# The out stage of a streaming-encoder block: VectorE forms the sums of m's blocks, and the low parts move between the additions

## The reference

```
merged = g_sb * y_sb + g_gla * y_gla
x = x + jnp.einsum('bsd,de->bse', merged, w_out[layer])
return _rmsnorm(x, g_final)
```

## Time and profile before

| | us |
|---|---|
| median of 3 runs | 820.55 (820.23 to 822.45) |
| the profiled execution, its own time | 820.71 |
| its span | 818.6 |
| TensorE busy, share of the span | 793.8, 97% |
| VectorE busy | 580.9, 71% |
| ScalarE busy | 410.5, 50% |
| GpSimd busy | 50.6, 6% |
| mean granted TensorE clock | 0.994 of full |

### The profile page before, as it was taken

How to read it: one execution, slowest core, us unless ns; L and a number is a source line. 1 busy time by engine, 2 the same in 40 slices (tenths; PEclk the granted TensorE clock), 3 DMA queues, 4 the chain that set the end, 5 groups by cost and what they waited for, 6 DMA issues and landing times.

```text
span 818.6 us, 11843 instructions
## 1 busy us (share of the span) xinstructions
PE 793.8 (97%) x4441; PEld 664.0 (81%) x4441; DVE 580.9 (71%) x811; ACT 410.5 (50%) x706; POOL 50.6 (6%) x44
## 2 busy tenths in 40 slices
PE   5999999999999999999999999999999999999896
PEld 5778888888888888879889888888888888888685
DVE  6528896989698698946645656665467776778865
ACT  8536675756666465655254153344343333465432
POOL 1630000000000000020000000000000000012500
PEclk9999999999999999999999999999999999999899
DMA  9852011112110220021110001234433344384222
GB/s 321 286 200 52 26 40 40 49 42 60 35 41 26 52 51 26 27 78 53 44 36 26 26 29 52 86 134 138 143 116 104 109 129 128 132 304 175 103 104 102
DMA packets 72483, 76.31 MB, mean 93 GB/s; under 512 B 3804, under 2 KB 57207, under 8 KB 71928
## 3 DMA queue, kind: packets, MB, share of 16 engines
q1 hardware_dynamic: 72386, 75.71, 28.8%
q10 hardware_dynamic: 54, 0.01, 0.0%
HBM read 55.79 MB, written 15.73 MB: 87 GB/s over the span
## 4 chain that ended last, share of the span: by engine, by line
PE 79%; DVE 10%; issue 5%; ACT 4%; POOL 1%; DMA 0%; DVEq 0%; ACTq 0%; POOLq 0%
PE pj L715 22%; PE tr L1019 5%; PE ob L967 5%; PE sc L967 5%; PE pj L859 4%; PE pj L1019 4%; PE ob L1019 4%; DVE surv L1680 4%; PE ob L807 3%; PE sc L1019 3%; PE pj L731 3%; PE tr L817 3%; PE pj L840 3%; PE sc L784 2%; PE tr L1077 2%
## 5 line engine op out<-in xcount | busy, mean ns | idle before, releaser
L715 PE MATMUL pj<-h_hi,w_lo 128*128 128x512 f32 x336 | 134.1, 399 | 0.0
L715 PE MATMUL pj<-h_hi,w_hi 128*128 128x512 f32 x336 | 133.8, 398 | 0.0
L715 PE MATMUL pj<-h_lo,w_hi 128*128 128x512 f32 x336 | 133.6, 398 | 0.0
L1680 DVE TENSOR_TENSOR_SCAN surv<-surv 128x128 f32<-128x128 f32 (+3 forms) x64 | 86.4, 1350 | 19.2 <-ACT beta L1186 18.7
L715 PEld LDWEIGHTS pj<-h_hi,w_lo 128*128 128x128 f32 x336 | 63.5, 189 | 12.1 <-issue 0.5
L715 PEld LDWEIGHTS pj<-h_lo,w_hi 128*128 128x128 f32 x336 | 63.3, 188 | 12.0 <-issue 0.3
L715 PEld LDWEIGHTS pj<-h_hi,w_hi 128*128 128x128 f32 x336 | 63.5, 189 | 11.7 <-issue 0.2
L1227 ACT ACTIVATE wt_hi<-tr 128x512 fp32r<-128x512 f32 (+2 forms) x96 | 43.6, 490 | 43.2 <-PE tr L817 41.7
L1603 DVE TENSOR_TENSOR w_lo<-w_raw,w_hi 128x1024 fp32r<-128x1024 f32 x33 | 40.3, 1221 | 26.7 <-ACT w_hi L1119 26.5
L1725 DVE TENSOR_TENSOR wt_lo<-tr,wt_hi 128x512 fp32r<-128x512 f32 (+2 forms) x96 | 50.0, 548 | 5.3 <-ACT wt_hi L1227 4.8
L1683 DVE TENSOR_TENSOR beta<-beta,surv 128x128 f32<-128x128 f32 (+3 forms) x64 | 48.5, 758 | 2.2
(11 more groups left out here) (400 smaller groups left out, 1932.5 us busy)
## 6 DMA issues: line engine op xcount, KB each, us to landing
w_raw<-in_w_in SPq DMA_DIRECT2D x30, 512.0 KB, 3.6
y_scratch<-y_ring SPq DMA_DIRECT2D x28, 256.0 KB, 2.0
graw<-in_w_in SPq DMA_DIRECT2D x14, 512.0 KB, 4.6
y_back<-y_scratch SPq DMA_DIRECT2D x14, 512.0 KB, 5.1
x_t<-in_x SPq DMA_DIRECT2D x8, 512.0 KB, 6.2
wrow<-in_w_out SPq DMA_DIRECT2D x4, 1024.0 KB, 7.6
w_scratch<-wsum SPq DMA_DIRECT2D x4, 1024.0 KB, 4.7
wout_raw<-in_w_out SPq DMA_DIRECT2D x8, 512.0 KB, 6.9
```

Source lines behind the costliest of these rows:

```text
L715: mm = pe.matmul(pj[bank][:, :], (w_lo if p == 2 else w_hi)[:, slot, k, :], (h_lo if p == 1 else h_hi)[:, k, HALF * h:HALF * h + HALF], st ...
L1680: dve.tensor_tensor_scan(s[:, ::-1], s[:, ::-1], s[:, ::-1], 1.0, ALU.mult, ALU.bypass)\
```

## The change

GpSimd keeps only the broadcast of `g_final`, now behind a wait for `mt_lo` 3 (the low part of pair 0's second row tile) instead of one for m. VectorE gets the four sums of each item as `item_sums(p, part)`. The order on VectorE and ScalarE is rewritten: `low_tw` comes in the order 3, 1, 0, 2; `row_sum(2)`, `row_sum(3)` and the two `norm_row` of pair 0 go into item 0's part of the loop, and the low parts of products 4, 5, 6 too. ScalarE makes tw[2] last of the four and both `square` of pair 0 behind all high parts of item 0. Each `square` from the third on waits for `rstd5`. Line breaks that change nothing are left out.

```diff
 # GpSimd
-            pool.wait_ge(m_ready, 2)
-            pool.wait_ge(m_step, 3 * NP + 5)
-            for p in range(WHOLE_PAIRS, 4):
...
-                pool.tensor_tensor(o12, o12, os2[:, :, :], ALU.subtract).then_inc(os_ready, 1)
+            pool.wait_ge(fin_loaded, 16)
+            pool.wait_ge(mt_lo, 3)
+            pool.partition_broadcast(g_fin[:, :], g_fin_row[0:1, :], P).then_inc(fin_bc, 1)
 # TensorE
-            TW_LOW = {1: 2, 3: 8, 4: 6, 5: 4}
+            TW_LOW = {1: 2, 3: 6, 4: 4, 5: 8}
 # ScalarE
+                if n >= 2:
+                    act.wait_ge(rstd5, n - 1)
...
-            high_tw(2)
             high_tw(1)
-            act.wait_ge(fin_bc, 1)
-            act.wait_ge(o5_free, 3)
-            square(0, 0)
             high_tw(0)
             high_out(1, 5)
             high_out(1, 4)
             high_out(1, 6)
+            high_tw(2)
+            act.wait_ge(fin_bc, 1)
+            act.wait_ge(o5_free, 3)
+            square(0, 0)
             act.wait_ge(o5_free, 4)
             square(1, 1)
 # VectorE
-            row_sum(0)
+            def item_sums(p, part):
+
+                a, b = slice(2 * P * p, 2 * P * p + P), slice(2 * P * p + P, 2 * P * p + 2 * P)
+                o11, o21, o12, o22 = mT[:, 4:KT, a], mT[:, 4:KT, b], mT[:, 0:4, a], mT[:, 0:4, b]
+                n = p - WHOLE_PAIRS
+                if part == 0:
+                    if n == 0:
+                        dve.wait_ge(m_step, 3 * NP + 5)
+                    else:
+                        dve.wait_ge(om_low, NP * n)
+                    dve.tensor_tensor(os3[:, :, :], o11, o21, ALU.subtract).then_inc(os_ready, 1)
+                    dve.wait_ge(os_ready, 4 * n + 1)
+                    dve.tensor_tensor(o21, o21, o22, ALU.add).then_inc(os_ready, 1)
+                else:
+                    dve.wait_ge(os_ready, 4 * n + 2)
+                    if n == 0:
+                        dve.wait_ge(o5_ready, 4 * WHOLE_PAIRS)
+                    dve.tensor_tensor(os2[:, :, :], o21, o11, ALU.subtract).then_inc(os_ready, 1)
+                    dve.wait_ge(os_ready, 4 * n + 3)
+                    dve.wait_ge(om_low, NP * n + 1)
+                    dve.tensor_tensor(o12, o12, os2[:, :, :], ALU.subtract).then_inc(os_ready, 1)
+
+            item_sums(1, 0)
             low_out(1, 0, 0)
             low_out(1, 1, 1)
-            row_sum(1)
             low_tw(3, 0)
             low_out(1, 2, 2)
-            row_sum(2)
             low_out(1, 3, 3)
-            low_tw(2, 2)
-            low_tw(1, 4)
-            row_sum(3)
-            low_tw(0, 6)
-            low_out(1, 4, 5)
-            low_out(1, 5, 4)
-            low_out(1, 6, 6)
+            row_sum(0)
+            row_sum(1)
+            low_tw(1, 2)
+            item_sums(1, 1)
+            low_tw(0, 4)
...
+                if n == 0:
+                    low_out(1, 4, 5)
+                    low_out(1, 5, 4)
                 gather(2, xb2, xb2, banks[3], ALU.subtract, 0)
-                next_low(0)
-                next_low(1)
+                if n == 0:
+                    low_out(1, 6, 6)
+                else:
+                    next_low(0)
+                    next_low(1)
                 gather(3, xa1, banks[1], xa1, ALU.add, 1)
                 if n == 0:
-                    dve.wait_ge(fin_bc, 1)
-                for m in range(2):
-                    if n == 0:
-                        if p == 1 or m:
-                            norm_row(2 * p - 2 + m, 2 * ((p - 1) % 2) + m)
-                    else:
+                    low_tw(2, 6)
+                    gather(4, xb2, banks[2], xb2, ALU.add, 2)
+                    row_sum(2)
+                    row_sum(3)
+                    next_low(0)
+                    next_low(1)
+                    next_low(2)
+                else:
+                    for m in range(2):
                         norm_row(2 * p - 2 + m, 2 * ((p - 1) % 2) + 1 - m)
-                next_low(2)
-                gather(4, xb2, banks[2], xb2, ALU.add, 2)
+                    next_low(2)
+                    gather(4, xb2, banks[2], xb2, ALU.add, 2)
...
+                else:
+                    item_sums(p + 1, 0)
                 next_low(3)
                 dve.wait_ge(u2_copied, n + 1)
                 gather(5, xa2, o_sum[:, :], xa2, ALU.add, 0)
+                if p < 3:
+                    item_sums(p + 1, 1)
                 next_low(4)
...
                 next_low(5)
+                if n == 0:
+                    dve.wait_ge(fin_bc, 1)
+                    norm_row(0, 0)
+                    norm_row(1, 1)
                 gather(7, xa2, banks[2], xa2, ALU.add, 5)
                 next_low(6)
```

More of the change, by code:

```diff
@@ L1508, in square @@
             def square(n, row):
-                act.activation(junk5[:, :], x_res[:, row, :], ACT.Square, accum_out=stats[:, 48 + n % 2:49 + n % 2])                    .then_inc(ss5, 1)
+                if n >= 2:
+                    act.wait_ge(rstd5, n - 1)
+                act.activation(junk5[:, :], x_res[:, row, :], ACT.Square, accum_out=stats[:, 48 + n % 2:49 + n % 2])\
+                    .then_inc(ss5, 1)
                 act.wait_ge(ss5, 2 * n + 1)
@@ L1558, in _ @@
             act.wait_ge(pair_step, done + 3)
-            act.activation(junk5[:, 0:HALF], x_res[:, 2, 0:HALF], ACT.Square, accum_out=stats[:, 54:55])                .then_inc(ss5, 1)
+            act.activation(junk5[:, 0:HALF], x_res[:, 2, 0:HALF], ACT.Square, accum_out=stats[:, 54:55])\
+                .then_inc(ss5, 1)
             copy_u2(3)
@@ L1564, in _ @@
             act.wait_ge(ss5, ss + 2)
-            act.activation(stats[:, 50:51], stats[:, 48:49], ACT.Sqrt, bias=stats[:, 63:64], scale=1.0 / D)                .then_inc(ss5, 1)
+            act.activation(stats[:, 50:51], stats[:, 48:49], ACT.Sqrt, bias=stats[:, 63:64], scale=1.0 / D)\
+                .then_inc(ss5, 1)
             act.wait_ge(pair_step, done + 9)
-            act.activation(junk5[:, HALF:D], x_res[:, 2, HALF:D], ACT.Square, accum_out=stats[:, 55:56])                .then_inc(ss5, 1)
+            act.activation(junk5[:, HALF:D], x_res[:, 2, HALF:D], ACT.Square, accum_out=stats[:, 55:56])\
+                .then_inc(ss5, 1)
             act.wait_ge(tail_step, 1)
             act.wait_ge(ss5, ss + 4)
-            act.activation(stats[:, 51:52], stats[:, 55:56], ACT.Sqrt, bias=stats[:, 56:57], scale=1.0 / D)                .then_inc(ss5, 1)
+            act.activation(stats[:, 51:52], stats[:, 55:56], ACT.Sqrt, bias=stats[:, 56:57], scale=1.0 / D)\
+                .then_inc(ss5, 1)
             act.wait_ge(rstd5, ST)
             act.wait_ge(tail_step, 2)
-            act.activation(x_res[:, 2, 0:HALF], x_res[:, 2, 0:HALF], ACT.Copy, scale=stats[:, 53:54])                .then_inc(tail_out, 1)
+            act.activation(x_res[:, 2, 0:HALF], x_res[:, 2, 0:HALF], ACT.Copy, scale=stats[:, 53:54])\
+                .then_inc(tail_out, 1)
         @block.vector
@@ L2097, in low_out @@
                 dve.wait_ge(om_high, NP * (p - WHOLE_PAIRS) + nth + 1)
-                dve.tensor_tensor(om_lo[o][:, :, :], out_source(p, o), om_hi[o][:, :, :].bitcast(F32), ALU.subtract)                    .then_inc(om_low, 1)
+                dve.tensor_tensor(om_lo[o][:, :, :], out_source(p, o), om_hi[o][:, :, :].bitcast(F32), ALU.subtract)\
+                    .then_inc(om_low, 1)
             def low_tw(n, high_done):
@@ L2168, in _ @@
                 gather(1, xa1, banks[0], xa1, ALU.add, 0)
+                if n == 0:
+                    low_out(1, 4, 5)
+                    low_out(1, 5, 4)
                 gather(2, xb2, xb2, banks[3], ALU.subtract, 0)
[L2170 to L2171 removed]
+                if n == 0:
[3 more added lines that the diff above has]
+                    next_low(1)
                 gather(3, xa1, banks[1], xa1, ALU.add, 1)
                 if n == 0:
[L2174 to L2179 removed]
+                    low_tw(2, 6)
[7 more added lines that the diff above has]
+                    for m in range(2):
                         norm_row(2 * p - 2 + m, 2 * ((p - 1) % 2) + 1 - m)
[L2181 to L2182 removed]
+                    next_low(2)
+                    gather(4, xb2, banks[2], xb2, ALU.add, 2)
                 if p == 3:
                     dve.wait_ge(ss5, 13)
[L2185 removed]
+                    dve.tensor_scalar(stats[:, 56:57], stats[:, 54:55], 1.0 / D, EPS, ALU.mult, ALU.add)\
+                        .then_inc(tail_step, 1)
                     dve.tensor_tensor(xa1, xa1, g_fin[:, 0:HALF], ALU.mult).then_inc(tail_step, 1)
+                else:
+                    item_sums(p + 1, 0)
                 next_low(3)
```

## The result

The changed kernel takes 827.07 us in the median (826.72 to 828.09, 4 runs), the kernel before 821.2 (820.23 to 822.45, 4 runs). The ratio is 1.0069, with a 95% interval of 1.0052 to 1.0087: slower by 0.7%. The profiled execution is the longest of the four, 828.09 us; its span is 826.4.

What follows compares the result with a forecast made beforehand. TensorE, 97% busy, was taken to bound the kernel, with one wait in the out stage. From the profiled 820.71 us, -6.92 + 10.45 + 2.68 = +6.2 gave 826.9, stated as 826.8 us; range 821.0 to 829.0.

Steps and rivals of the forecast that it cites:

- first pause: TensorE before product 4 of item 0, waiting for `gather(3)`: 4.24 us late before the change, claimed to go.
- VectorE stands for item 1's first high part: VectorE waits 4.3 us because ScalarE's high parts for item 1 stand behind both squares of pair 0.
- half clock behind it: TensorE after item 1's late product 4: matmuls at half clock cost 2.68 us, bounds 0 to 1 us more.
- The estimate for a store: From the Trainium skill's DMA figures, a 512 KB store takes 3.2 us; with two loads at 4.4, half a us more.
- The first term: Item 0 on TensorE: the wait before product 4 and the half clock after it go, -6.92 us.
- The second term: TensorE before item 1's product 4: a new wait of 10.45 us for x of pair 2, plus 2.68 of half clock.
- Part 3: Items 1 and 2 and the tail: `os2`, pair 3's x, `square` waits and the broadcast cost nothing more.
- the pause that just goes: Rival: item 0's wait on TensorE goes and nothing takes its place, 813.8 us; chance 0.08.
- The chain without ScalarE's 4.3 us: Rival: item 1's product 4 still waits, but VectorE doesn't stand still for high parts, 821.6 to 822.3 us; chance 0.15.
- The third: Rival: item 0's wait stays in part as a low part or tw[0] comes late, 828 to 831 us; chance 0.09.

Runs made afterwards that it cites:

- experiment 2: The changed kernel with the high parts of item 1's products 0 to 2 ahead of pair 0's two squares on ScalarE: 823.18 us, ratio 1.0026.
- experiment 6: The kernel before with only the two `norm_row` of pair 0 late, behind low part 5 of item 1, squares waiting for `rstd5`: 827.08 us, ratio 1.0086.
- experiment 7: The changed kernel with pair 0's row sums, squares and `norm_row` early, and the four sums back on GpSimd behind the broadcast: 817.2 us, ratio 0.9962.
- experiment 1: The changed kernel with pair 0's `row_sum(2)`, `row_sum(3)`, squares and `norm_row` moved early, sums still on VectorE: 813.97 us, ratio 0.9916.
- experiment 4: The kernel before with GpSimd's broadcast of `g_final` ahead of item 0's four sums, which stay on GpSimd: 819.48 us, ratio 0.9985.
- experiment 5: The kernel before with only the sums moved to VectorE; low parts, row sums, squares and `norm_row` where they were: 815.69 us, ratio 0.9947.
- experiment 3: The changed kernel without the load of x for pair 2, `gather(1)` of item 1 waiting for pair 0's stores instead: 822.09 us, ratio 1.0014.

## Why the prediction was right

It said 826.8 us, and 827.07 was measured. That this is within 0.3 us is partly luck: the forecast was 6.25 us over a before of 820.55, and the measured one is 5.87 over a before of 821.2. The two sides of the sum have to be looked at one by one, since a sum of large terms can come right by chance. With the 1.27 us of the trace's later start taken off:

| step | forecast | trace of the changed kernel |
|---|---|---|
| first pause | gone | gone |
| `gather(3)` of item 0 ends | 756.55 | 756.53 |
| `square(0, 0)` starts | 760.1 | 760.10 |
| VectorE stands for item 1's first high part | 4.3 | 4.18 |
| second `norm_row` of pair 0 ends | 777.6 | 777.50 |
| pair 2's loads go out | 780.3 | 780.25 |
| `gather(1)` of item 1 starts | 784.7 | 784.69 |
| product 4 of item 1 restarts | 787.85 | 787.84 |
| half clock behind it | 2.68 | 2.97 |

So the terms are -6.92 + 10.44 + 2.97 = +6.49, against +6.2 foretold and 6.53 between the out stages of the two traces. The bounds of the unknown terms were not used up: the load took 4.44 us from issue to use within the 4.2 to 6.0 given (4.71, 4.46 and 4.46 in experiments 2, 6 and 7). One term had no bounds and should have had them: the 2.72 us from the last `norm_row` to the loads. It came out at 2.75, but was 4.61 in experiment 1, and 3.49 for pair 1 in the changed kernel; at such a value the pause would have been 0.7 to 1.9 us longer. The estimate for a store that the prediction set beside its sum, half a us longer, was too long.

*The first term* (-6.92) was right, by a reason that was only partly right. The text laid the pause on GpSimd's idle time around the broadcast and named the contention as a second thing. Experiment 4 shows that taking the idle time away from `os2` alone gives back 1.6 of 6.92 us; experiment 5, which takes both away, 5.6 (it leaves 1.14 + 0.14). Each hides the other in part, and a single chain of waits cannot show that.

*The second term* was taken apart by experiments 1 to 3: with `norm_row` early there is no pause, with ScalarE's order turned 3.7 us of it go, without the load 4.45. The rest, by the trace, is the 2.75 us of the stores and VectorE's own work ahead of `norm_row`. Experiment 6 shows a pause of the same kind, 4.30 us, with the sums left on GpSimd, so a late `norm_row` is enough to make one.

*Part 3* held: nothing else was late, and the time from item 2's first product to the end of the span is 26.16 us, against 26.12.

*One step failed*, without weight. The broadcast was foretold 5.7 us behind its wait, beside the last `wout_low`. It came at once and stretched an operation of the merge instead (1.39 us, 0.42 elsewhere in the stage). The cost of 0.97 was right, the place was not, and in both places it is covered.

The rivals: the pause that just goes (813.8) is what experiment 1 gives, 813.97, once `norm_row` stands early; the reason against it, the x of pair 2 being ten us late, was the right one. The chain without ScalarE's 4.3 us was priced 821.6 to 822.3 and experiment 2 gave 823.18; the price left out that the squares then hold product 3's high part, that the load can take 4.71 us, and that the half clock is 2.97. The third, a first pause that stays in part, did not occur: `gather(3)` of item 0 ended 1.83 us before product 4 started, where 1.8 to spare had been forecast.

## What to carry to other kernels

An instruction that frees a buffer is not a tail of its item: find who refills the buffer and who reads that, add the store, the load and the consumer's own steps up, and place it by that date. Here a `norm_row` that TensorE never waits for directly had 10.3 us of hidden chain behind it (stores 2.75, load 4.44, three gathers and two low parts 3.1). So its own date was 10.3 us ahead of product 4, and moving it behind work that was needed later than that, such as the low parts of products 3 to 5, cost all that the rest of the change had gained, and 5.9 us more. When an engine's order is rewritten, walk every engine past the first repaired wait, up to the next product that was not waiting before: every due time comes earlier by what was gained (6.92 us here), and a transfer that had been in time by less than that comes late.

## What the runs showed of the hardware

**A pause of 2.2 us can cost the clock.** The mean granted clock behind experiment 4's pause of 2.21 us, and what stands before it:

```profile
core 0: us, PE busy (x) PEld busy (x) DVE busy (x) ACT busy (x) POOL busy (x), PEclk, DMA share, GB/s
756.50:758.40 1.90, 0.01 (x1) 0.01 (x1) 1.90 (x3) 1.87 (x5) 0.00 (x0) 1.00 0.00 0
758.40:764.00 5.60, 5.39 (x15) 3.98 (x16) 5.57 (x10) 0.96 (x3) 4.22 (x3) 0.70 0.00 0
758.40:760.00 1.60, 1.60 (x4) 1.30 (x5) 1.60 (x3) 0.75 (x2) 0.38 (x1) 0.57 0.00 0
760.00:762.00 2.00, 2.00 (x6) 1.53 (x5) 2.00 (x5) 0.00 (x0) 1.92 (x2) 0.50 0.00 0
762.00:764.00 2.00, 1.79 (x7) 1.16 (x7) 1.97 (x4) 0.21 (x1) 1.92 (x2) 0.99 0.00 0
```

The clock was full during the pause, fell just behind its end, and was full again from about 762. Product 3 took 4.81 us up to the start of the next, of which 0.21 is a wait, so the price is 1.9. Collected, with the restart in it: idle 2.21 us cost 1.9; 4.07 cost 2.68 (before), 3.96 and 4.14 cost 2.63 and 1.67 (experiment 6), 5.83 cost 2.95, 6.56 cost 2.97 and 10.27 cost 2.97. An idle 0.98 us cost 0.14, all of it restart at full clock (experiment 5). So in these traces the price hardly grows with the pause above 5 us, and it varies by 1 us at about 4. Each is one trace; experiment 3's runs, which spread by 2.5 us, may hold cheaper ones.

**Contention with GpSimd is large for VectorE's work with two inputs in SBUF.** Besides, a scaling of 1.28 us took 2.35 (experiment 6), the two halves of a `low_tw`, 2.35 us, took 3.95 (experiment 7). A gather that reads one input from PSUM kept its 0.68 us beside the same sums (758.50 in experiment 7). The Trainium skill (SBUF — State Buffer, on the shared port pair) describes it as a lock that one holds for a whole instruction. Experiment 6 agrees roughly: the scaling took 1.07 us more, and the GpSimd sum that ran when it started (774.58 to 775.88) had 1.27 us left.

**GpSimd's idle time around the broadcast.** 5.72 and 8.18 us in the trace of before, 7.14 and 7.20 between broadcast and first sum where the broadcast stands first, 0.22 ahead of a broadcast that follows a rest of 368 us. Part of this is waiting for inputs: 5.65 of the 8.18 come after pair 0's last product (747.7), and 5.2 of the 7.14 after the write of m that the first sum needs (735.31). No record in the profile says what it is; it was not taken apart further.
